# A ring of six gathered rows instead of eight, and its freed weight slot used to keep projection pieces

## The chip, the cores and the metric

The kernel runs on one core of a Trainium2 chip. A core has TensorE (PE, with its weight loads as PEld), VectorE (DVE), ScalarE (ACT), GpSimd (POOL) and SyncE (SP), each with an instruction stream of its own, and 16 DMA engines that all of them share. The metric is the device time of one execution in microseconds.

## What is computed

A first block of two layers and a second block of four, on 256 tokens of 1024 features, all in 32-bit floats. The change lies in the first block, whose layers are an attention, a layer norm, an expert layer and a layer norm. Layer 0 has differential attention with the output projection `w_o_a`, layer 1 stick-breaking attention with `w_o_b`. The expert layer of either one is

```python
def _peer(x, w_pq, sub_keys, u, v):
    q = (xt @ w_pq).reshape(T, PEER_HEADS, 2, PEER_HALF)
    scores = jnp.einsum('thcd,hckd->thck', q, sub_keys)
    ...
    u_sel = jnp.take(u, idb, axis=0)
    h = jax.nn.gelu(jnp.einsum('td,ted->te', xblk, u_sel), approximate=False)
    v_sel = jnp.take(v, idb, axis=0)
    return jnp.einsum('te,ted->td', gb * h, v_sel)
```

So each token takes 128 rows of u and of v, 1024 numbers each, from a table of 16384 experts. The second block (three kinds of attention and a squared-ReLU MLP) follows and is not touched.

## The kernel before, in words

**The expert stage.** The tokens lie in two tiles of 128, and there are two layers, which makes four windows (`WINDOWS`) of 128 picks (`SEL`): 512 picks. For each pick POOL issues one indirect DMA (`gathers`, L2902), which brings for all 128 tokens of the tile the row of u and v of one chosen expert, 128 x 2048 numbers, 1 MB. It goes into the next slot of a ring (`gathered`, `GATHER_SLOTS` = 8). VectorE multiplies the u half by x and sums it (`product`, L2386), ScalarE takes the gelu of two picks at a time (`activate`, L1876), VectorE multiplies it by the gates (L2399), ScalarE writes the two weights as diagonal matrices (`make_diagonal`, L1882), and TensorE adds diagonal times v half to two accumulators (`mix`, L1439), a pair of picks per step. POOL may issue pick n when pick n - 8 is mixed (`value_mixed`), and it issues in order. A window has 64 pairs.

**Work between the pairs.** Every engine runs the same list of pairs, and constants say which other step stands next to which pair. In window 0 that is the attention of layer 0 for the second tile (`second_step`); in windows 1 and 2 the stick-breaking attention of layer 1 for tile 0 and tile 1 (`stick_step`). Windows 0 to 2 also have `late_step`: at pairs 35 to 38 the output projection in four pieces of 256 columns (`s.o`), at 47 to 50 the queries of the next expert layer in four pieces (`s.peer_q`), at 52 its scores. Window 3 has the first input projection of the second block.

**Where weights lie.** `weights` has four slots of 2 MB. The ring of eight takes slots 1 and 2 (two rows each) and four rows in `arena`. Slot 0 is split into two halves for `Piece`, a piece of 1 MB that SP loads shortly before its use and that frees its half when used. Slot 3 holds `KeptPiece`s, first two query pieces of layer 0 (`peer_chunks[1]`), then two output pieces of layer 1 (`kept_o`), loaded once and used for two tiles. `PlacedPiece`s lie in two more places outside of `weights` (`kept_places`): output pieces 2 and 3, of layer 0 and then of layer 1.

**Order of the transfers.** SP issues all weight loads in one fixed order (the function of `@block.sync`), and waits ahead of each for the last user of its place, so one that waits holds up those behind it. `load_stick` loads `Piece`s, `load_kept` the placed ones, `load_chunks` whole chunks. The gathers go out on POOL's queue, at the same 16 DMA engines. `ring_free` says for which projection blocks the first gathers wait, because at the start the ring's places still hold weights of layer 0. At the end of the stage `slot_release` says after which pick each slot takes the first chunks of the second block (the seam); `chunks[1]` (slot 3) is loaded only after the last gather has landed (L1006), and then those of slots 2 and 1 follow (L998).

Of the kernel before, what the change touches and what calls it, by code (L numbers as in the profile page):

```python
# [82 lines left out]


ROW = 2 * D
GATHER_SLOTS = 8
PAIRS = TOPK // 2


# [136 lines left out]
def build(nc, A, out):  # L226
    es = ExitStack()
    with es:
# [24 lines left out]
        arena = sb("arena", [P, 8 * D])  # L253

        in_arena = [arena[:, n * ROW:(n + 1) * ROW] for n in range(4)]
        in_slot = {slot: [weights[:, slot, n * ROW:(n + 1) * ROW] for n in range(2)] for slot in (1, 2)}
        gathered = in_slot[2] + in_arena + in_slot[1]
        assert len(gathered) == GATHER_SLOTS
        o = arena[:, 0:NT * 2 * D].rearrange("p (t d) -> p t d", t=NT)
        bias8 = arena[:, NT * 2 * D:NT * 2 * D + HEADS * T].rearrange("p (h k) -> p h k", h=HEADS)  # L260
# [212 lines left out]
        def in_weights(flat, n, slot, g):  # L473

            slot_uses[slot] += 1
            return halved_chunk(flat, n, weights[:, slot, :], weight_loaded[slot], 16 * slot_uses[slot], (psum_filled[g.bank], g.filled))
# [145 lines left out]
        def column_pieces(flat, first):  # L622

            return [src for src, _, _ in chunks_laid_out(flat, 2 * D, PIECE_COLS)[first:first + 4]]
# [11 lines left out]
        class Second:  # L636
# [3 lines left out]
            def __init__(self):  # L640
                self.t, self.norm, self.keys = 1, (0, 1), 16
                self.block = diff_block(1, 0, 2)
                self.turn = diff_turned(1, (3, 4, 5, 6))
                n = HEADS // 2
                self.probs0, self.done0 = probs_ready.plan(HEADS), unit_done.plan(n)
                self.s, self.turned = [], []
                for j in range(n):
                    self.s.append([group(2 + m) for m in range(2)])
                    self.turned.append(group(4 + j % 2))
                self.values = [group(6 + j % 2, fill=False) for j in range(n // 2)]  # L650
                self.o_turn = maps_turned(1, (4, 5))
                self.out = self.o_turn.done
                half_release[:] = [(psum_filled[self.block[-1].bank], self.block[-1].filled)] * 2
                self.o = [Piece(src, n, 2 + n % 2) for n, src in enumerate(column_pieces(A["w_o_a"][0], 0)[0:2])]
                self.o += [PlacedPiece(n, 1, 2 + n) for n in range(2)]
                self.rows = plan_rows()
                self.peer_turn = Turn(turn_tile(x, xT, 1), (2, 3))
                self.peer_q = [Piece(src, n, 2 + n % 2) for n, src in enumerate(column_pieces(A["peer_w_q"][0], 0)[0:2])]
                self.peer_q += [KeptPiece(peer_chunks[1], n, 2 + n) for n in range(2)]
                self.scores = [group(4 + b) for b in range(4)]  # L660

        class Stick:
# [3 lines left out]
            def __init__(self, t):  # L666
                self.t, self.norm, self.keys, banks = t, (2, t), 32, (2 * t, 2 * t + 1)
                self.n = 4 if t == 0 else 8
                self.log0, self.soft0 = stick_log_ready.plan(self.n), stick_soft_ready.plan(self.n)
                self.e0, self.done0, self.zeroed0 = stick_e_ready.plan(self.n), unit_done.plan(self.n), zeroed.plan(2)  # L670
                self.x_turn = Turn(turn_tile(x, xT, t), banks)
                keys, values = (column_pieces(A["w_kv_b"][0], first) for first in (0, 4))
                queries = column_pieces(A["w_q_b"][0], 0)
                self.k, self.q, self.v, self.pieces = [], [], [], []
                for n in range(4):
                    for kind, src in ((self.k, keys), (self.q, queries), (self.v, values)):
                        kind.append(Piece(src[n], len(self.pieces), banks[0]))
                        self.pieces.append(kind[-1])
                self.s = [group(4 + b % 2) for b in range(self.n)]
                self.later = [group((6, banks[1])[b % 2]) for b in range(self.n)]  # L680
                self.out = [group(7, fill=False) for _ in range(2)]
                first = len(self.pieces)
                self.o = [KeptPiece(kept_o, n, banks[n]) for n in range(2)]
                self.o += [PlacedPiece(n, 2, banks[n]) for n in range(2)]
                self.rows = plan_rows()
                self.peer_turn = Turn(turn_tile(x, xT, t), banks)
                self.peer_q = [Piece(src, first + n, banks[n % 2]) for n, src in enumerate(column_pieces(A["peer_w_q"][1], 0))]
                self.scores = [group(4 + b) for b in range(4)]

            def heads(self, b):  # L690
# [43 lines left out]
        def plan_mixed(w):  # L734

            return [group(2 * (w % NT) + half, fill=False) for half in range(2)]
# [42 lines left out]
        peer_scores += [group(5), group(6)]  # L779


        ring_free = {0: diff_out_blocks[1][-1], 2: later_blocks[4][-1], 4: later_blocks[5][-1], 6: later_blocks[1][-1]}

        ln_root, ln_done = {}, {}
        diff_root = [root_asked.plan()]
# [6 lines left out]
        mixed, ln_in = [plan_mixed(0)], {}  # L792
        second = Second()
        kept_o = in_weights(A["w_o_b"][0], 0, 3, second.peer_q[3].group)
        mixed.append(plan_mixed(1))
        ln_in[EARLY_RUNS[0]] = plan_rows()
        stick = [Stick(0)]
# [6 lines left out]
        for s in late:  # L804
            ln_in[s.norm] = s.rows
        scores_at = [peer_scores] + [s.scores for s in late]
        slot_release[0] = half_release[1 - stick[1].peer_q[0].half]
        kept_until = stick[1].o[1].group
        slot_release[3] = (psum_filled[kept_until.bank], kept_until.filled)
        for slot, buffers in ((1, (6, 7)), (2, (0, 1))):  # L810
            picks = [n for n in range(WINDOWS * SEL) if n % GATHER_SLOTS in buffers]
            slot_release[slot] = (value_mixed.sem, picks[-1] + 1)
        early_normed = y[:, :, 2 * D:3 * D]
        early_in = TileProjection(chunks_laid_out(A["a_w_in"][0], A_IN), (0, 3, 2, 1), (0, 1, 2, 3))
        early_turn = Turn(turn_tile(early_normed, xT, 0), (4, 5))
# [173 lines left out]
        def _(sp):  # L989
# [44 lines left out]
            def load_stick(pieces):  # L1034
                for c in pieces:
                    sp.wait_ge(*c.after)
                    sp.dma_start(c.view, c.src).then_inc(piece_loaded[c.half], 16)
# [34 lines left out]
            load_chunks(peer_chunks)  # L1072
            load_ln_rows()
            sp.wait_ge(x_ready, 1)
            load_kept(0, A["w_o_a"][0], 2)
            queried = peer_q[0]
            sp.wait_ge(psum_filled[queried.bank], queried.filled)
            sp.wait_ge(bias_written, 16)
            load_kept(1, A["w_o_a"][0], 3)
            load_stick(second.o[0:2])  # L1080
            load_stick(second.peer_q[0:2])
            scored = second.scores[3]
            sp.wait_ge(psum_filled[scored.bank], scored.filled)
# [1 line left out]
            for s in stick:  # L1085
                load_stick(s.pieces[0:2])
                if s.t == 0:
                    load_chunks([kept_o])
                    for n in range(2):
                        used = second.o[2 + n].group  # L1090
                        sp.wait_ge(psum_filled[used.bank], used.filled)
                        load_kept(n, A["w_o_b"][0], 2 + n)
                load_stick(s.pieces[2:])
                load_stick(s.peer_q)

            scored = stick[1].scores[3]
            sp.wait_ge(psum_freed[scored.bank], scored.freed)
# [1930 lines left out]
```

## Time and profile before

| | us |
|---|---|
| three runs: median (lowest to highest) | 2735.91 (2732.36 to 2737.7) |
| the profiled execution | 2735.13 |
| its span on the core | 2733.3 |
| TensorE busy in the span | 2513.3 (92%) |
| VectorE busy | 1758.9 (64%) |
| ScalarE busy | 995.4 (36%) |
| GpSimd busy | 651.8 (24%) |
| share of 16 DMA engines taken by POOL's queue | 48.2% |
| share taken by SP's queue | 24.0% |

The span runs from the first to the last instruction of the one execution that was profiled; all durations and instants below are of it. A wait is idle time of an engine, put down to whatever ended it. The landing time of a DMA is counted from the start of its issue to its completion.

### The profile page before, as it was taken

To read this page: it belongs to the slowest core of one execution; us is meant where nothing else is said; L and a number is where in the kernel's file an instruction comes from. 1 tells how busy PE (TensorE), PEld (TensorE's weight loads), DVE (VectorE), ACT (ScalarE), POOL (GpSimd) and SP (SyncE) were. 2 spreads that over 40 slices of the span, in tenths; PEclk is the share of its full clock that TensorE was granted. 3 is DMA by queue.
4 is the path that set the end of the run, shared out by engine and by line. 5 is a ranking of instruction groups with operands and counts; after the bars stand their busy time and mean duration, and the time that the engine had idled before them with its cause. 6 is when DMAs were issued, how large, how long until landed. Compare 5 with 4: busy or idle time off the path is not lost.

```text
span 2733.3 us, 29518 instructions
## 1 busy us (share of the span) xinstructions
PE 2513.3 (92%) x10053; PEld 1581.4 (58%) x10053; DVE 1758.9 (64%) x3966; ACT 995.4 (36%) x2016; POOL 651.8 (24%) x636
## 2 busy tenths in 40 slices
PE   8989897898988899978977899999999999999999
PEld 4544453464553565533422357885688668865787
DVE  2668875756758667678776566554666546647654
ACT  2136332334322354223222144433544444424443
POOL 0134443433434324444444120001000110002000
PEclk9999999999999999999999999999999999999999
DMA  7699999999999999999999734543253405523452
GB/s 296 238 378 415 417 410 402 421 421 421 387 421 421 421 391 406 403 418 421 421 422 421 319 124 154 187 158 147 78 212 140 187 32 204 194 106 124 155 193 98
DMA packets 111344, 791.69 MB, mean 290 GB/s; under 512 B 12979, under 2 KB 15686, under 8 KB 19958
## 3 DMA queue, kind: packets, MB, share of 16 engines
q0 software_dynamic: 74464, 540.07, 48.2%
q1 hardware_dynamic: 36758, 250.10, 24.0%
q8 instruction: 63, 1.03, 0.1%
q14 instruction: 59, 0.48, 0.0%
HBM read 789.05 MB, written 4.22 MB: 290 GB/s over the span
## 4 chain that ended last, share of the span: by engine, by line
PE 65%; DMA 18%; DVE 11%; ACT 3%; issue 2%; POOL 1%; SPq 0%; DVEq 0%; ACTq 0%; POOLq 0%
PE psum L1439 15%; PE psum L1553 13%; PE psum L1160 11%; DMA arena<-in_peer_uv,scratch 10%; PE psum L1510 8%; DMA weights<-in_peer_uv,scratch 7%; PE psum L1512 4%; PE psum L1246 3%; DVE weights L2386 2%; PE psum L1254 2%; DVE arena L2386 2%; PE psum L1232 1%; PE psum L1137 1%; PE psum L1221 1%; PE psum L1208 1%
## 5 line engine op out<-in xcount | busy, mean ns | idle before, releaser
L1439 PE MATMUL psum<-weights,scratch 128*128 128x512 f32 x1024 | 479.4, 615 | 79.0 <-ACT scratch L1882 79.0
L1439 PE MATMUL psum<-arena,scratch 128*128 128x512 f32 x1024 | 476.0, 610 | 74.6 <-ACT scratch L1882 74.4
L2748 DVE TENSOR_TENSOR piece<-weights,piece 128x2048 fp32r<-128x2048 f32 x128 | 292.0, 2292 | 181.1 <-ACT piece L1974 181.1
L2386 DVE SCALAR_TENSOR_TENSOR arena<-arena,x 128x1024 f32<-128x1024 f32 x256 | 309.8, 1223 | 146.5 <-DMA arena<-in_peer_uv,scratch 145.1
L2902 POOL DMA_INDIRECT weights<-in_peer_uv,scratch x256 | 289.0, 1129 | 460.5 <-PE psum L1439 406.0
L2386 DVE SCALAR_TENSOR_TENSOR weights<-weights,x 128x1024 f32<-128x1024 f32 x256 | 309.4, 1225 | 132.4 <-DMA weights<-in_peer_uv,scratch 129.1
L1439 PEld LDWEIGHTS psum<-weights,scratch 128*128 128x128 f32 x1024 | 192.5, 195 | 330.0 <-issue 209.7
L2902 POOL DMA_INDIRECT arena<-in_peer_uv,scratch x256 | 280.3, 1095 | 408.8 <-PE psum L1439 397.3
L1439 PEld LDWEIGHTS psum<-arena,scratch 128*128 128x128 f32 x1024 | 190.9, 193 | 322.5 <-issue 198.8
L1553 PE MATMUL psum<-piece,hidden 128*128 128x512 f32 x1536 | 358.9, 390 | 0.0
L1876 ACT ACTIVATE scratch<-scratch 128x2 f32<-128x2 f32 x255 | 51.9, 203 | 840.2 <-DVE arena L2386 420.4
L1160 PE MATMUL psum<-weights,xT 128*128 128x512 f32 (+2 forms) x792 | 334.4, 576 | 17.7 <-DMA weights<-in_w_qkv_a 8.2
L1553 PEld LDWEIGHTS psum<-piece,hidden 128*128 128x128 f32 x1536 | 284.3, 188 | 59.6
L1510 PE MATMUL psum<-split_x,piece 128*128 128x512 f32 x896 | 318.6, 398 | 0.0
L1974 ACT ACTIVATE piece<-weights 128x2048 fp32r<-128x2048 f32 x128 | 242.7, 1907 | 127.1 <-PE psum L1512 127.1
L1512 PE MATMUL psum<-split_x,piece 128*128 128x256 f32 x896 | 251.5, 281 | 0.0
L1160 PEld LDWEIGHTS psum<-weights,xT 128*128 128x128 f32 x792 | 147.0, 192 | 177.3 <-issue 163.6
L1882 ACT ACTIVATE scratch<-const,scratch 128x128 f32<-128x128 f32 x512 | 178.0, 394 | 63.8 <-DVE scratch L2399 57.0
L1510 PEld LDWEIGHTS psum<-split_x,piece 128*128 128x128 f32 x896 | 168.4, 188 | 41.1
L1512 PEld LDWEIGHTS psum<-split_x,piece 128*128 128x128 f32 x896 | 169.2, 189 | 2.0
L1993 ACT ACTIVATE hidden<-scratch 128x512 fp32r<-128x512 f32 x64 | 40.5, 632 | 218.3 <-DVE scratch L2769 198.8
L1246 PEld LDWEIGHTS psum<-xT,weights 128*128 128x128 f32 x896 | 105.7, 194 | 17.0 <-issue 16.3
(273 smaller groups left out, 2686.8 us busy)
## 6 DMA issues: line engine op xcount, KB each, us to landing
weights<-in_w_up SPq DMA_DIRECT2D x64, 1024.0 KB, 4.8
weights<-in_w_down SPq DMA_DIRECT2D x64, 1024.0 KB, 4.8
weights<-in_w_kv_b SPq DMA_DIRECT2D x16, 1024.0 KB, 9.4
weights<-in_peer_w_q SPq DMA_DIRECT2D x10, 1024.0 KB, 9.2
weights<-in_a_w_in SPq DMA_DIRECT2D x5, 2048.0 KB, 11.5
weights<-in_w_q_b SPq DMA_DIRECT2D x8, 1024.0 KB, 9.2
weights<-in_a_w_out SPq DMA_DIRECT2D x4, 2048.0 KB, 8.6
weights<-in_w_qkv_a SPq DMA_DIRECT2D x3, 2048.0 KB, 16.9
```

The source lines that it names most:

```text
L1160: mm = pe.matmul(psum[g.bank][:, 0:w], source[:, block0 + k, t * P:(t + 1) * P], c.columns(k, c0, w), start=(k == 0), stop=(k == c.rows - 1))
L1246: mm = pe.matmul(to[:, j * P:(j + 1) * P], c.columns(k, j * P, P), xT[:, k, t * P:(t + 1) * P], start=(k == 0), stop=(k == KB - 1))
L1254: mm = pe.matmul(to[:, 0:PIECE_COLS], xT[:, k, t * P:(t + 1) * P], c.columns(k), start=(k == 0), stop=(k == KB - 1))
L1439: mm = pe.matmul(psum[g.bank][:, :], diagonal[:, n % DIAGONALS, :], row[:, D + half * BANK:D + (half + 1) * BANK], start=(k == 0), stop=(k ...
L1510: pe.matmul(psum[g.bank][:, 0:2 * T], w[0][:, k, b * P:(b + 1) * P], split_x_pair[:, k, :, :], start=(k == 0), stop=False)
L1512: mm = pe.matmul(psum[g.bank][:, 0:T], w[1][:, k, b * P:(b + 1) * P], split_x[0][:, k, :], start=False, stop=(k == KB - 1))
L1553: mm = pe.matmul(psum[g.bank][:, :], h[a][:, k, t * P:(t + 1) * P], w[c][:, k, half * BANK:(half + 1) * BANK], start=(first and k == 0 and ...
L1882: act.activation(diagonal[:, n % DIAGONALS, :], identity, ACT.Copy, scale=weight[:, k:k + 1])\
L1974: act.activation(split_piece[n][0][:, :], raw_piece[n], ACT.Copy).then_inc(high_ready.sem, 1)
L2386: dve.scalar_tensor_tensor(u, u, 1.0, x[:, n // SEL % NT, :], ALU.mult, ALU.mult, accum_out=dots[:, n % SEL:n % SEL + 1]).then_inc(dotted. ...
L2748: dve.tensor_tensor(split_piece[n][1][:, :], raw_piece[n], split_piece[n][0][:, :], ALU.subtract)\
L2902: pool.indirect_dma_start(gathered[n % GATHER_SLOTS], None, rows, bass.IndirectOffsetOnAxis(ap=expert[:, w % NT, k:k + 1], axis=0), elemen ...
```

## The change

The ring has six rows: four in `arena` and two in slot 1. Slot 2 is no longer part of it and holds two pieces, each used more than once. At first it keeps output columns 512 to 1023 of layer 0 (`diff_out_chunks[1]`, which was loaded there for tile 0 anyway) for the second tile as well; the two places outside take output pieces 0 and 1 instead of 2 and 3, and the two `Piece` loads of pieces 0 and 1 go. After the last of them is used, SP loads query pieces 0 and 1 of the second expert layer into slot 2 (`kept_q`, one transfer of 2 MB, ahead of `kept_o`); both stick tiles use them, and only query pieces 2 and 3 are still loaded per tile. Before, each tile loaded all four. POOL waits for pick n - 6 instead of n - 8. The first gathers wait for `later_blocks[4]`, `[5]` and `[1]`. At the end slot 2 is free when the second tile's query piece 1 is used, and slot 1 at the last pick of ring places 4 and 5, pick 509, for which it waits until 510 picks are mixed; before, these were 512 mixed for slot 1 and a late pick for slot 2.

```diff
-GATHER_SLOTS = 8
+GATHER_SLOTS = 6
...
-        in_slot = {slot: [weights[:, slot, n * ROW:(n + 1) * ROW] for n in range(2)] for slot in (1, 2)}
-        gathered = in_slot[2] + in_arena + in_slot[1]
+        in_slot = [weights[:, 1, n * ROW:(n + 1) * ROW] for n in range(2)]
+        gathered = in_arena + in_slot
...
-                self.o = [Piece(src, n, 2 + n % 2) for n, src in enumerate(column_pieces(A["w_o_a"][0], 0)[0:2])]
-                self.o += [PlacedPiece(n, 1, 2 + n) for n in range(2)]
+                self.o = [PlacedPiece(n, 1, 2 + n) for n in range(2)]
+                self.o += [KeptPiece(diff_out_chunks[1], n, 2 + n) for n in range(2)]
...
-                self.peer_q = [Piece(src, first + n, banks[n % 2]) for n, src in enumerate(column_pieces(A["peer_w_q"][1], 0))]
+                self.peer_q = [KeptPiece(kept_q, n, banks[n]) for n in range(2)]
+                self.peer_q += [Piece(src, first + n, banks[n]) for n, src in enumerate(column_pieces(A["peer_w_q"][1], 0)[2:4])]
...
-        ring_free = {0: diff_out_blocks[1][-1], 2: later_blocks[4][-1], 4: later_blocks[5][-1], 6: later_blocks[1][-1]}
+        ring_free = {0: later_blocks[4][-1], 2: later_blocks[5][-1], 4: later_blocks[1][-1]}
...
+        kept_q = in_weights(A["peer_w_q"][1], 0, 2, second.o[3].group)
...
-        slot_release[0] = half_release[1 - stick[1].peer_q[0].half]
+        slot_release[0] = half_release[stick[1].peer_q[3].half]
...
-        for slot, buffers in ((1, (6, 7)), (2, (0, 1))):
-            picks = [n for n in range(WINDOWS * SEL) if n % GATHER_SLOTS in buffers]
-            slot_release[slot] = (value_mixed.sem, picks[-1] + 1)
+        queried_until = stick[1].peer_q[1].group
+        slot_release[2] = (psum_filled[queried_until.bank], queried_until.filled)
+        in_slot_1 = [n for n in range(WINDOWS * SEL) if n % GATHER_SLOTS in (4, 5)]
+        slot_release[1] = (value_mixed.sem, in_slot_1[-1] + 1)
...
-            load_kept(0, A["w_o_a"][0], 2)
+            load_kept(0, A["w_o_a"][0], 0)
...
-            load_kept(1, A["w_o_a"][0], 3)
-            load_stick(second.o[0:2])
+            load_kept(1, A["w_o_a"][0], 1)
...
-                    load_chunks([kept_o])
+                    load_chunks([kept_q, kept_o])
                     for n in range(2):
-                        used = second.o[2 + n].group
+                        used = second.o[n].group
...
-                load_stick(s.peer_q)
+                load_stick(s.peer_q[2:])
```

## Rows read from the trace of the kernel before

**Rows 1.** The page: its head, and GB/s in 40 equal slices of the span

```profile
span 2733.3 us, 29518 instructions
...
GB/s 296 238 378 415 417 410 402 421 421 421 387 421 421 421 391 406 403 418 421 421 422 421 319 124 154 187 158 147 78 212 140 187 32 204 194 106 124 155 193 98
```

**Rows 2.** Windows: busy us of each engine, granted clock, DMA share, GB/s; 150:1530

```profile
150.00:1530.00 1380.00, 1210.59 (x3997) 633.45 (x3996) 987.25 (x2522) 463.68 (x1105) 563.92 (x507) 0.98 1.01 413
```

**Rows 3.** Waits, 123:1545: engine and line, releaser, us in total, times, longest

```profile
DVE arena L2386 <- DMA arena<-in_peer_uv,scratch: 145.1, 123, 3.4
...
DVE weights L2386 <- DMA weights<-in_peer_uv,scratch: 129.1, 107, 3.7
...
PE psum L1439 <- ACT scratch L1882: 153.4, 110, 6.2
```

**Rows 4.** Timeline, 1521:1544: start us, us, engine, line, op, out<-in

```profile
1523.66 0.94 POOL L2902 DMA_INDIRECT arena<-in_peer_uv,scratch  x1 [0.78 <-PE psum L1439]
...
1524.64 3.70 PE L1439 MATMUL psum<-weights,scratch 128*128 128x512 f32 x8 [1.25 <-ACT scratch L1882]
...
1528.61 0.94 POOL L2902 DMA_INDIRECT weights<-in_peer_uv,scratch  x1 [0.78 <-PE psum L1439]
...
1537.40 1.23 DVE L2386 SCALAR_TENSOR_TENSOR arena<-arena,x 128x1024 f32<-128x1024 f32 x1 [1.25 <-DMA arena<-in_peer_uv,scratch]
...
1539.56 3.70 PE L1439 MATMUL psum<-arena,scratch 128*128 128x512 f32 x8 [1.28 <-ACT scratch L1882]
```

**Rows 5.** Source L2902, seven windows starting at 122, 180, 340, 400, 700, 960, 1080

```profile
DMA to landing us min/median/max: 5.5/11.6/16.9
DMA to landing us min/median/max: 6.6/10.2/13.9
DMA to landing us min/median/max: 6.7/8.7/11.3
DMA to landing us min/median/max: 5.6/9.5/13.4
DMA to landing us min/median/max: 5.5/8.6/12.6
DMA to landing us min/median/max: 7.3/9.5/13.6
DMA to landing us min/median/max: 5.7/8.4/10.7
```

**Rows 6.** Timeline, POOL, 735:748; landings of the gathers issued at 727.6, 737.3, 743.2

```profile
737.32 1.05 POOL L2902 DMA_INDIRECT weights<-in_peer_uv,scratch  x1 [0.30 <-issue]
...
743.18 0.93 POOL L2902 DMA_INDIRECT arena<-in_peer_uv,scratch  x1 [2.26 <-issue]
...
DMA to landing us min/median/max: 7.4/7.4/7.4
DMA to landing us min/median/max: 9.2/9.2/9.2
DMA to landing us min/median/max: 8.3/8.3/8.3
```

**Rows 7.** Source L2902, three windows: 1120:1190, 1200:1290, 750:900

```profile
DMA to landing us min/median/max: 9.7/14.3/18.6
DMA to landing us min/median/max: 9.6/12.6/13.7
DMA to landing us min/median/max: 11.1/13.5/19.4
```

**Rows 8.** Timeline, SP (its DMA issues), 100:1560

```profile
162.00 1.02 SPq L1037 DMA_DIRECT2D weights<-in_w_o_a  x2
...
424.43 0.44 SPq L998 DMA_DIRECT2D weights<-in_w_o_b  x1
...
646.05 127.95 SPq L1037 DMA_DIRECT2D weights<-in_peer_w_q  x4
```

**Rows 9.** Windows, columns as in rows 2; 765:790

```profile
765.00:790.00 25.00, 25.00 (x141) 17.90 (x140) 9.68 (x18) 3.49 (x12) 7.63 (x7) 1.00 1.01 420
```

## The prediction

> **What bounds the kernel now.** I read the page's head and its line of GB/s first. The span is 2733.3 us, and from the third to the twenty-second of the forty slices the DMA engines move 378 to 422 GB/s, mostly 421; before and after they move far less [rows 1]. That plateau is the expert stage, in which 512 gathers of 1 MB each (a row of u and v per token) pass through the ring. Over its inner 1380 us the engines are busy for 1.01 of the time, at 413 GB/s, while TensorE is busy 1210.59 us [rows 2]. So 421 GB/s is the ceiling here, one gather (1.05 MB) costs 2.49 us of it, a pair 4.98 us, and the stage is 8/421, or 1.9%, from the ceiling. The list of waits agrees: VectorE stands 145.1 + 129.1 us for gathers that have not landed, TensorE 153.4 us for the diagonals that follow from them [rows 3]. TensorE is a close second, so there are places where it leads and the DMA follows; the change has to be read there.
>
> **The loop through the ring.** The timeline of the quiet end of the stage shows one turn. A gather is issued at 1523.66; its product starts at 1537.40, as soon as it has landed, 13.74 us after the issue; its pair is mixed from 1539.56 for 3.70 us, to 1543.26, which is 5.86 us after the landing. An earlier pair's mix ends at 1528.34 (1524.64 + 3.70), and the next issue into the slot that it freed is at 1528.61, 0.27 us later [rows 4]. The turn is 13.74 + 5.86 + 0.27 = 19.87 us, four pairs of 4.97 us. Of the 13.74 us most is waiting behind other gathers: a gather into an empty queue lands in 5.5 us (the first line of [rows 5]), its pair's second, issued just behind it, in 7.4 [rows 6]. That surplus is what eight slots buy.
>
> **Six slots in the steady part.** The turn becomes three pairs, 14.91 us, and leaves 14.91 - 5.86 - 0.27 = 8.8 us for the landing of a pair's second gather. Enough? The nearest rows are a place where the queue had just run low: seconds issued at 737.32 and 743.18 land after 9.2 and 8.3 us, at 746.5 and 751.5, 5.0 us apart [rows 6], which is the full rate. So 8.8 us keeps the pace, and I charge the steady part 0. Lower bound 0 (the ceiling is not lifted); upper bound, if 9.2 were needed instead of 8.8, 0.4 us for each 14.9 us over some 700 us of steady stretches: 19 us.
>
> **Six slots where the queue runs low.** When TensorE or VectorE leads for a while, gathers land sooner and sooner after their issue, since slots come back late. The lowest landing time of a stretch less the 5.5 us of an empty queue is its spare; two slots fewer take one pair, 4.98 us, from it, and what is missing is time in which the DMA engines stand still. After each such stretch the DMA leads again, so it is not won back. The stretches from 122, 180, 340, 400, 700, 960 and 1080 us have minima, in that order, of 5.5, 6.6, 6.7, 5.6, 5.5, 7.3 and 5.7 [rows 5]. Without the first, the losses are 3.9 + 3.8 + 4.9 + 5.0 + 3.2 + 4.8 = 25.6 us. Two milder ones, from 1120 and 1200, have 9.7 and 9.6 (the first two lines of [rows 7]): 0.8 + 0.9 = 1.7. Together 27.3 us. Each term lies between 0 (the dip was TensorE's to lose) and 4.98.
>
> The stretch from 180 to 300 deserves more. Its median landing is 10.2 us (second line of [rows 5]), not 13.7: the second tile's attention holds the rows some 3.5 us longer in every turn. A turn of 14.9 us less that longer hold (19.9 - 10.2 = 9.7) leaves 5.2, under both 5.5 and 7.4. At 1.3 us missing (to 6.5, the middle of those two) in eight turns of 14.9 us it would lose 10 us, against 3.9 charged; VectorE's own work hides part of it. I take 8, that is 4 more; bounds 0 and 6 more.
>
> **Loads taken away and moved.** All pass through the same engines, 2.49 us per MB. (a) The two output pieces loaded at 162.00 [rows 8] are no longer needed: 5.0 us less. They follow the first dip (5.5 us at the start of the stage, where two rows fewer are fetched ahead, a loss of 5.0), and the next dip comes from 180 on. The gain and the first dip's loss cancel: 0. The first gather also starts later, after the block for which the third used to wait, which no row prices; the same head start of the DMA covers it, or it falls in that term. (b) SP now issues kept_q (2 MB) next to kept_o in the burst that begins around 424.43 [rows 8]. It is waited for by its queries only some 300 us on, but it goes through full engines just when that burst already holds the gathers back, and SP has nothing else queued behind it but the rest of the burst: +5.0 us, bounds 0 and 5.0. (c) Of each of the two sets of four query pieces of the second expert layer (the third line of [rows 8] is the first set, 646.05 to 774) two go, 5.0 us of engine time each. The last two of the set stood in the query steps around 766, where TensorE is busy 25.00 of 25.00 us with the DMA still at 420 GB/s [rows 9]. There the ring is full, and what the loads leave free the gathers can't use beyond the spare. The minimum from 750 to 900 is 11.1 (third line of [rows 7]), a spare of 5.6: 4.98 of the ring and 4.98 saved leave 4.4 idle, a net gain of 0.6. In the second set (stretch from 1120, spare 4.2) saving 5.0 makes 5.0 more idle: 0. So 4 MB fewer buy 0.6 us there; bounds 0 and 10.
>
> **Edits at nothing.** The output pieces in the kept places and in slot 2 have landed long before use (the former second set did the same); TensorE's waits for them are on semaphores already reached. If that cover failed, it would stand one landing of a loaded queue, 9 to 14 us, once. The instructions on all engines and their order stay. At the seam the last weight chunk is freed by pick 510 instead of 512; SP issues it at most one mix, 3.70 us [rows 4], earlier, but behind two chunks on the same engines: 0, bounds -2 and 0.
>
> **The sum.** 27.3 + 4.0 + 0 + 5.0 - 0.6 + 0 = 35.7 us. The profiled execution took 2735.13 us (span 2733.3 and 1.8 around it), 0.8 below the median of the runs shown, 2735.91: 2735.1 + 35.7 = 2770.8, rounded to 2771 us.
>
> **A rule against this.** The rows put an unloaded gather at 5.5 us. The Trainium skill, "DMA: Bandwidth & Descriptors", section "Anatomy of one DMA — SWDGE (gpsimd) path", gives about 2.0 us plus the bytes at 436 GB/s, 4.4 us for 1 MB. By that rule a pair in flight would hide the fixed part and six slots would be ample; every dip would have 1.1 us more to spare, which lowers the sum by some 8 us. The rows, 5.5 and 7.4, are of this access and decide. The rule's own outcome is rival 1.
>
> **Rivals.** (1) The queue never really empties: six slots cover the landing everywhere, the dips belong to TensorE and not to the DMA, and the stage simply moves 4 MB less: 4 x 2.49 = 10 us, 2725 us. It decides if the GB/s in the dips stay as they are. For it: the engines' share stays near 1.00 even in most dips. Against it: landing times of 5.5, 5.6 and 5.7 us are those of an empty queue, and the GB/s fell to 387 and 391 in such slices [rows 1]. Chance 0.07. (2) About half of the dips are given back, since TensorE leads on both sides of them, and kept_q hides: 27.3/2 + 4 - 3 (part of the saved loads) = about 15 us, 2750 us. For it: the dips of 340 and 400 lie close together, as do those of 960 and 1080. Chance 0.17. (3) The steady part starves too, since a turn has no room for VectorE's routing steps: the 19 us bound above on top of the sum, 2790 us. For it: the margin is 8.8 against 8.3 to 9.2. Against it: the steady row of seconds at 8.3 keeps the pace. Chance 0.16. (4) Gains and losses cancel: loads save 10, dips cost 10, 2735 us. Chance 0.04. The forecast keeps 0.56.
>
> **How the numbers follow.** A measurement of this kernel can't tell less than about 0.2% (5.5 us) from no change. Faster 0.07 is rival 1, same 0.04 rival 4, slower 0.89 the rest. The range: from 2747 (rival 2 less 3 us) to 2800 (rival 3 with the upper bound of the attention stretch and some of the dips at 4.98); rivals 1 and 4 and the tail above 2800 are left out, under 2 in 10.
>
> **What would show it.** The profile after should have the same instructions and busy times, a stage longer by 30 to 40 us with about 4 MB less, so GB/s near 400 instead of 413; landing times with minima of 5.5 in all of the dips and steady ones of 8 to 9 instead of 13 us; steady pairs still 4.97 us apart. Behind the seam nothing changes. Landing minima well above 5.5 in the dips would prove rival 1 or 2; steady pairs of 5.1 us or more rival 3. The forecast is wrong if the stage's length moves by under 10 us although the landing times fall to 5.5, or if kept_q's burst stretches nothing.

## The result, and the profile after

The changed kernel takes 2831.92 us, the median of four runs (2826.11 to 2838.07), beside 2735.81 us for the kernel before (2732.36 to 2737.7): a ratio of 1.0356, interval 1.0337 to 1.0374. The change makes the kernel 96 us slower; forecast were 36 us slower, and the time lies 32 us above the range. The execution that was profiled took 2838.07 us, with a span of 2836.2 us, 102.9 more than before [rows 1].

The page of the changed kernel: its head, the granted TensorE clock and the GB/s in 40 slices, and the two groups of the mixing matmuls.

```profile
span 2836.2 us, 29513 instructions
...
PEclk9988899899999999999999999999999999999999
...
GB/s 286 246 317 336 354 343 373 404 407 417 377 367 398 385 395 390 353 370 400 385 399 415 414 202 119 208 177 141 84 191 192 105 90 192 180 143 119 134 192 104
...
L1441 PE MATMUL psum<-arena,scratch 128*128 128x512 f32 x1368 | 665.5, 633 | 139.0 <-ACT scratch L1884 137.6
...
L1441 PE MATMUL psum<-weights,scratch 128*128 128x512 f32 x680 | 324.6, 622 | 64.8 <-ACT scratch L1884 64.6
```

The plateau of 421 GB/s of [rows 1] is gone: slices 3 to 7 are at 317 to 373. The work is the same: 2048 matmul records of the mix before and after. But they are busy 665.5 + 324.6 = 990.1 us, where the page of the kernel before has 479.4 + 476.0 = 955.4, and the clock digit falls to 8 in four of the first eight slices.

Windows over the whole expert stage, first the changed kernel, then the one before (columns as in [rows 2]):

```profile
123.00:1648.00 1525.00, 1285.70 (x4145) 664.41 (x4144) 1017.11 (x2591) 471.81 (x1130) 591.52 (x516) 0.96 0.96 379
```

```profile
123.00:1547.00 1424.00, 1250.05 (x4146) 654.78 (x4144) 1010.76 (x2589) 474.29 (x1130) 572.89 (x516) 0.98 1.00 410
```

The DMA engines move 379 instead of 410 GB/s, over 1525 instead of 1424 us. The list of waits for the stage, changed kernel, answers [rows 3]:

```profile
DVE arena L2388 <- DMA arena<-in_peer_uv,scratch: 266.8, 211, 4.4
...
PE psum L1441 <- ACT scratch L1884: 202.1, 120, 5.2
...
DVE weights L2388 <- DMA weights<-in_peer_uv,scratch: 126.9, 98, 3.7
```

VectorE waits 266.8 + 126.9 = 393.7 us for rows, 119.5 more than before; TensorE waits 202.1 us for diagonals, 48.7 more. The chain at the seam (the hand-over from the last gathers to the first weights of the second block) shows that the difference ends there; first after, then before:

```profile
1645.96 11.58 DMA weights<-in_a_w_in
...
1657.59 2.84 PE psum L1162 x6
```

```profile
1543.16 11.49 DMA weights<-in_a_w_in
...
1554.69 7.13 PE psum L1160 x16
```

The first projection behind the gathers starts at 1657.59 and at 1554.69, 102.9 us apart, which is the whole difference of the spans. So the question is one of the stage alone.

**The quiet end.** The timeline of the changed kernel answers [rows 4]:

```profile
1572.00 3.70 PE L1441 MATMUL psum<-arena,scratch 128*128 128x512 f32 x8 [1.62 <-ACT scratch L1884]
...
1575.97 0.94 POOL L2904 DMA_INDIRECT arena<-in_peer_uv,scratch  x1 [0.78 <-PE psum L1441]
...
1584.76 1.22 DVE L2388 SCALAR_TENSOR_TENSOR arena<-arena,x 128x1024 f32<-128x1024 f32 x1 [1.25 <-DMA arena<-in_peer_uv,scratch]
...
1586.91 3.70 PE L1441 MATMUL psum<-arena,scratch 128*128 128x512 f32 x8 [1.27 <-ACT scratch L1884]
...
1590.89 0.94 POOL L2904 DMA_INDIRECT arena<-in_peer_uv,scratch  x1 [0.78 <-PE psum L1441]
```

A mix ends at 1575.70, its slot is issued into at 1575.97, the product of that row starts at 1584.76, its pair is mixed to 1590.61, and at 1590.89 the slot is issued into again. The turn is 14.92 us, three pairs of 4.97; from issue to product it is 8.79 us where it was 13.74. This is the forecast's steady turn to the tenth of a us. Most of the loss lies elsewhere.

**Where it lies.** The table takes the ends of the mixes from both traces and divides by pairs (a window is 64 pairs); the next columns are means over the second gathers of the pairs, from the start of the issue to the start of the product, and from there to the end of the mix.

| pairs | us a pair, before | after | issue to product, before | after | product to mixed, before | after |
|---|---|---|---|---|---|---|
| 8 to 32 | 5.17 | 6.05 | 11.7 | 9.2 | 8.4 | 8.8 |
| 32 to 56 | 5.23 | 6.15 | 11.5 | 8.9 | 10.1 | 9.2 |
| 64 to 104 | 5.97 | 6.12 | 15.1 | 10.1 | 8.3 | 8.0 |
| 104 to 128 | 5.27 | 5.62 | 13.4 | 9.4 | 7.4 | 6.9 |
| 128 to 168 | 6.07 | 6.35 | 13.8 | 9.9 | 10.0 | 8.8 |
| 168 to 192 | 5.30 | 5.76 | 13.6 | 9.8 | 7.5 | 6.9 |
| 192 to 224 | 4.98 | 5.26 | 13.2 | 9.3 | 6.3 | 6.1 |
| 224 to 250 | 5.02 | 5.08 | 13.8 | 9.0 | 5.9 | 5.9 |

The rows of the table follow one identity: issue to product, plus product to mixed, plus about 0.4 us to the next issue, is 4 pairs before and 3 pairs after. For pairs 8 to 32 after that is 9.2 + 8.8 + 0.4 = 18.4, beside 3 x 6.05 = 18.2. The rows agree to some 0.3 us, but for pairs 32 to 56 before, 1 us off, since their turns end in the slower pairs behind. The identity holds whatever sets the pace, because POOL issues as soon as a slot is free. So it says how the parts of a turn add up and not which of them is the cause; that is what the experiments are for.

Pairs 56 to 64, beside SP's burst of loads, take 6.90 us before and 7.10 after. By window the loss is 55.4, 14.1, 21.9 and 11.4 us; the forecast had 21.6, 4.4, 8.8 and 0.9.

A piece of the attention stretch in the changed kernel, timeline from 231 to 266:

```profile
237.18 1.72 POOL L2904 DMA_INDIRECT weights<-in_peer_uv,scratch  x1 [0.78 <-PE psum L1441]
...
243.90 8.90 PE L1441 MATMUL psum<-arena,scratch 128*128 128x512 f32 x16
...
247.59 1.22 DVE L2388 SCALAR_TENSOR_TENSOR weights<-weights,x 128x1024 f32<-128x1024 f32 x1 [1.20 <-DMA weights<-in_peer_uv,scratch]
...
247.93 1.70 POOL L2904 DMA_INDIRECT arena<-in_peer_uv,scratch  x1 [9.04 <-PE psum L1441]
...
254.69 3.70 PE L1441 MATMUL psum<-weights,scratch 128*128 128x512 f32 x8
...
258.67 1.57 POOL L2904 DMA_INDIRECT weights<-in_peer_uv,scratch  x1 [0.78 <-PE psum L1441]
...
260.36 5.40 PE L1441 MATMUL psum<-arena,scratch 128*128 128x512 f32 x8 [1.97 <-ACT scratch L1884]
```

The gather issued at 237.18 is multiplied 10.4 us later, at 247.59, and mixed from 254.69 to 258.39, 10.8 us after that: TensorE mixes two pairs in one go (243.90, 8.90 us), then has attention steps, then mixes again. So slots come back in bunches: after 9.04 us in which POOL had none, it issues at 247.93. At 258.67 the slot of the gather of 237.18 is issued into again, a turn of 21.5 us. And the mix at 260.36, before which TensorE stood idle for 1.97 us, takes 5.40 us instead of 3.70: the granted clock over these 5.40 us is 0.68 of full speed, part of them at the lower level.

### The profile page after: what moved, and what is told of

Read it like the earlier page. It is cut to its first block, busy times and chain, and to the rows that moved or that the text cites. A ratio compares the mean times of both kernels' runs of the same rounds, so it can differ in the third digit from the quotient of the medians.

```text
span 2836.2 us, 29513 instructions
## 1 busy us (share of the span) xinstructions
PE 2549.8 (90%) x10053; PEld 1591.1 (56%) x10053; DVE 1764.7 (62%) x3966; ACT 993.4 (35%) x2016; POOL 670.4 (24%) x636
## 4 chain that ended last, share of the span: by engine, by line
PE 64%; DMA 19%; DVE 10%; ACT 4%; issue 2%; POOL 1%; SPq 0%; DVEq 0%; ACTq 0%; POOLq 0%
PE psum L1441 15%; DMA arena<-in_peer_uv,scratch 13%; PE psum L1555 12%; PE psum L1162 11%; PE psum L1512 7%; DMA weights<-in_peer_uv,scratch 5%; PE psum L1514 4%; PE psum L1248 3%; DVE arena L2388 3%; PE psum L1256 2%; PE psum L1139 1%; DVE weights L2388 1%; PE psum L1234 1%; ACT scratch L1884 1%; PE psum L1223 1%
## 5 line engine op out<-in xcount | busy, mean ns | idle before, releaser
L1441 PE MATMUL psum<-arena,scratch 128*128 128x512 f32 x1368 | 665.5, 633 | 139.0 <-ACT scratch L1884 137.6
L2388 DVE SCALAR_TENSOR_TENSOR arena<-arena,x 128x1024 f32<-128x1024 f32 x342 | 416.1, 1224 | 269.5 <-DMA arena<-in_peer_uv,scratch 266.8
L2904 POOL DMA_INDIRECT arena<-in_peer_uv,scratch x342 | 394.3, 1153 | 671.4 <-PE psum L1441 621.5
L1441 PEld LDWEIGHTS psum<-arena,scratch 128*128 128x128 f32 x1368 | 264.5, 201 | 490.2 <-issue 285.3
L1441 PE MATMUL psum<-weights,scratch 128*128 128x512 f32 x680 | 324.6, 622 | 64.8 <-ACT scratch L1884 64.6
L2388 DVE SCALAR_TENSOR_TENSOR weights<-weights,x 128x1024 f32<-128x1024 f32 x170 | 206.6, 1224 | 128.5 <-DMA weights<-in_peer_uv,scratch 126.9
L1441 PEld LDWEIGHTS psum<-weights,scratch 128*128 128x128 f32 x680 | 128.8, 197 | 237.8 <-issue 136.2
L2904 POOL DMA_INDIRECT weights<-in_peer_uv,scratch x170 | 193.5, 1138 | 287.2 <-PE psum L1441 267.8
```

The source lines that it names most:

```text
L1441: mm = pe.matmul(psum[g.bank][:, :], diagonal[:, n % DIAGONALS, :], row[:, D + half * BANK:D + (half + 1) * BANK], start=(k == 0), stop=(k ...
L2388: dve.scalar_tensor_tensor(u, u, 1.0, x[:, n // SEL % NT, :], ALU.mult, ALU.mult, accum_out=dots[:, n % SEL:n % SEL + 1]).then_inc(dotted. ...
L2904: pool.indirect_dma_start(gathered[n % GATHER_SLOTS], None, rows, bass.IndirectOffsetOnAxis(ap=expert[:, w % NT, k:k + 1], axis=0), elemen ...
```

## Experiments

All kernels differ from the one before or from the changed one by what their diff shows; where the depth of the ring changes, the lines that fit `ring_free` and `slot_release` to it are left out in part. Theory A, the turn: the time of a pair is the larger of the DMA ceiling and the turn of a slot divided by the pairs in the ring, where the turn has a landing part that can't shrink at will.

### The ring alone, and the loads alone

Six rows with the old loads, slot 2 idle:

```diff
-GATHER_SLOTS = 8
+GATHER_SLOTS = 6
...
-        gathered = in_slot[2] + in_arena + in_slot[1]
+        gathered = in_arena + in_slot
...
+        slot_release[2] = (psum_filled[diff_out_blocks[1][-1].bank], diff_out_blocks[1][-1].filled)
```

> The ring alone: six rows, and every weight load of the kernel before, in its old order and place; slot 2 stays idle in the stage. Theory A (turn): each slot now goes once through issue, landing, product, mixing in a turn that two fewer slots can no longer hide, and the time is the ring's alone: 2827 to 2837 us, with window 0 at 6.0 to 6.2 us a pair as in the changed kernel. Theory B (loads): kept_q's 2 MB in the burst near 424 us and the new places of the pieces cost what the forecast had not counted, so the ring alone is near the forecast: 2760 to 2780 us.

Measured 2835.18 us (2834.3 to 2836.07), ratio 1.0368 (1.0348 to 1.0389): the loss of the changed kernel, whole. In windows, 190 to 480 us, of before, the changed kernel and this one:

```profile
190.00:480.00 290.00, 252.37 (x822) 130.14 (x821) 217.80 (x576) 106.00 (x250) 119.77 (x106) 0.95 1.01 412
```

```profile
190.00:480.00 290.00, 250.24 (x797) 130.88 (x798) 193.82 (x499) 98.55 (x231) 110.85 (x94) 0.91 0.89 343
```

```profile
190.00:480.00 290.00, 247.12 (x798) 129.86 (x797) 192.99 (x495) 98.46 (x231) 107.99 (x95) 0.92 0.90 349
```

412 GB/s fall to 343 and 349, with about as many matmuls (822, 797 and 798 records). Two rows fewer are enough for the loss; the loads that were moved and saved are not needed for it.

The other half, eight rows and 6 MB fewer loads:

```diff
-                self.o = [Piece(src, n, 2 + n % 2) for n, src in enumerate(column_pieces(A["w_o_a"][0], 0)[0:2])]
+                self.o = [PlacedPiece(n, 1, 2 + n) for n in range(2)]
...
-                self.peer_q = [Piece(src, first + n, banks[n % 2]) for n, src in enumerate(column_pieces(A["peer_w_q"][1], 0))]
+                self.peer_q = [KeptPiece(kept_o, n, banks[n]) for n in range(2)]
+                self.peer_q += [Piece(src, first + n, banks[n]) for n, src in enumerate(column_pieces(A["peer_w_q"][1], 0)[2:4])]
...
-            load_stick(second.o[0:2])
...
-                load_stick(s.peer_q)
+                load_stick(s.peer_q[2:])
```

> The ring of eight with 6 MB of weight loads left out: the two output pieces of the diff layer and query pieces 0 and 1 of both stick tiles are not loaded, and the pieces already kept in their places are multiplied instead, so these columns of the output are computed from other weights. Theory A: such loads go where the ring is full or are absorbed by the next dip, 2725 to 2736 us. Rival: every MB is worth its 2.49 us in a stage that is bound by the DMA engines, 6 x 2.49 = 15 us, 2721 us or less.

Measured 2729.17 us (2725.72 to 2734.06), ratio 0.9982 (0.9972 to 0.9992): 5 us won (2.2 to 7.7) of the 15 that 6 MB take on the engines. The rival is out: loads that go out while the ring is full or ahead of a dip are worth about a third of their engine time together (a seventh to a half by the interval). What each of them is worth was not measured.

### Are the eight places or the waits of the ring what counts?

```diff
-                    if n >= GATHER_SLOTS:
-                        pool.wait_ge(value_mixed.sem, n - GATHER_SLOTS + 1)
-                    elif n in ring_free:
+                    if n >= GATHER_SLOTS - 2:
+                        pool.wait_ge(value_mixed.sem, n - (GATHER_SLOTS - 2) + 1)
+                    if n < GATHER_SLOTS and n in ring_free:
```

> The kernel before with its eight places, each gather still going where it went, but POOL waits until pick n - 6 is mixed instead of n - 8; all loads as before. Theory A (turn): the depth is what is waited for, so 2825 to 2840 us. Rival (fewer places in weights and more traffic in arena, or the later first gathers, cost part of it): clearly under 2820 us.

Measured 2831.45 us (2828.25 to 2834.64), ratio 1.035 (1.0329 to 1.0371). With every row in the place it had before and two gathers fewer on their way, the loss is all there. Neither the places nor the later start of the first gathers is needed for it, to within the some 5 us of the interval: over 190 to 480 us this kernel too moves 351 GB/s, with the engines busy 0.90 of the time.

### Seven rows and four

```diff
-GATHER_SLOTS = 8
+GATHER_SLOTS = 7
...
-        gathered = in_slot[2] + in_arena + in_slot[1]
+        gathered = in_slot[2][0:1] + in_arena + in_slot[1]
```

> The ring alone with seven rows, loads as before. Theory A (turn): a pair costs the larger of what it costs with eight rows and the turn divided by 3.5; the turn of the attention stretch is about 18.3 us in the changed kernel, 5.23 us a pair against 5.2 with eight rows, so seven rows lose little: 2740 to 2765 us. Rival (each dip loses what a row is worth, in proportion): half of what six rows lose, about 2784 us.

Measured 2761.8 us (2759.51 to 2764.1), ratio 1.01 (1.008 to 1.012): the seventh row is worth 73 us of the 100, the eighth 27. The loss is not in proportion.

```diff
-GATHER_SLOTS = 8
+GATHER_SLOTS = 4
...
-        gathered = in_slot[2] + in_arena + in_slot[1]
+        gathered = in_arena
```

> The ring alone with four rows. Theory A (turn): a pair costs half a turn. The part of the turn behind the start of the product and the issue was 9.1 to 9.5 us in the attention stretch, 8.4 and 9.2 in windows 1 and 2 and 6.5 in the quiet end with six rows; with a landing of 7.4 us for a pair in an empty queue that is 8.3, 7.9 to 8.3 and 7.0 us a pair, 465 us more than the changed kernel in the sum: 3250 to 3350 us. The forecast's own rule (each dip costs at most one more pair of rows, 4.98 us, and the steady part nothing down to an empty queue's landing) would give some 2890 us.

Measured 3317.94 us in one run. The turn gave 3250 to 3350, the forecast's own rule 2890. The single stretches scatter more than the sum: pairs 8 to 32 take 9.02 us and pairs 32 to 56 7.80, where 8.3 were expected for both. The same window (190 to 480) for seven and for four rows:

```profile
190.00:480.00 290.00, 244.43 (x808) 126.29 (x807) 207.20 (x544) 105.02 (x246) 116.75 (x102) 0.97 0.98 392
```

```profile
190.00:480.00 290.00, 192.86 (x488) 98.12 (x488) 145.68 (x381) 78.71 (x175) 64.88 (x66) 0.80 0.66 246
```

392 GB/s with seven, 246 with four, where the DMA engines work 0.66 of the time and the granted clock is 0.80. In the quiet end (pairs 224 to 250) the trace has 7.06 us a pair: 6.9 from issue to product, 6.9 on to the mixed pair and 0.4, half of a turn of some 14.1. From issue to product is now near the 7.4 us of [rows 6], and 7.0 to 8.2 in the stretches before; with six rows its mean never came under 8.9 in any row of the table. That is the number that the forecast had wrong.

### A delay that takes no DMA time

```diff
+                if n >= (WINDOWS - 1) * SEL and n % 2 == 0:
+                    for _ in range(4):
+                        act.wait_ge(act_step, then(act.activation(diagonal[:, n % DIAGONALS, :], identity, ACT.Copy,
+                                                                  scale=weight[:, k:k + 1])))
```

It stands in `make_diagonal` ahead of the real one; the result is the same. In the trace it is 1.70 us a pair (timeline of the ring of eight: the added writes, then the mix behind them):

```profile
1495.38 1.70 ACT L1884 ACTIVATE scratch<-const,scratch 128x128 f32<-128x128 f32 x4 [0.23 <-DVE scratch L2403]
...
1497.57 3.70 PE L1439 MATMUL psum<-weights,scratch 128*128 128x512 f32 x8 [1.27 <-ACT scratch L1886]
```

With eight rows:

> The kernel before, with a delay on ScalarE ahead of the first diagonal of each pair in window 3: the same diagonal is written four times more, each waited for, some 2 us a pair in all. It lengthens the way of every row from its landing to its mixing, and takes no DMA time and no time of TensorE. Theory A (turn): with eight rows the turn of the quiet end (19.9 us) holds a landing time of 13.7 us, of which an empty queue needs 7.4, so 2 us are hidden: 2733 to 2741 us. Rival (a delay on the way to the mix costs its length, or a fixed part of it, whatever the ring): 64 x 2 = 128 us or a large part of it, in both rings alike.

Measured 2734.52 us (2732.41 to 2743.14), ratio 0.9995 (0.9985 to 1.0005): nothing, for 64 x 1.7 = 109 us of added delay. With six rows:

> The changed kernel with the same delay in window 3. Theory A (turn): with six rows the turn is 14.9 us and its landing part 9.0, near its floor, so of each 2 us at least 0.4 and at most 2 come through, a third of them on every pair: 8 to 43 us more than the changed kernel, 2840 to 2875 us, while the same delay costs the ring of eight nothing. Rival (the steady part is bound by the DMA engines at either depth, as the forecast had it, and has room for 2 us): 2828 to 2836 us.

Measured 2863.37 us (2862.76 to 2874.91), ratio 1.048 (1.0454 to 1.0505): 31 us more than the changed kernel, 0.49 us for each of 64 pairs, a little under a third of 1.7 (0.57). Windows in the quiet end, eight rows (1420 to 1520) and six (1560 to 1640):

```profile
1420.00:1520.00 100.00, 75.06 (x160) 29.23 (x159) 63.54 (x145) 55.81 (x149) 48.47 (x41) 0.98 1.01 421
```

```profile
1560.00:1640.00 80.00, 59.42 (x114) 23.41 (x112) 44.41 (x99) 39.16 (x106) 32.12 (x29) 0.89 0.92 361
```

421 GB/s stand against 361. Without the delay the changed kernel has, at 1520 to 1600:

```profile
1520.00:1600.00 80.00, 58.52 (x128) 22.86 (x128) 51.73 (x120) 19.29 (x54) 34.65 (x32) 1.00 1.01 410
```

This is the cleanest test: the same 1.7 us is free in one ring and costs nearly its third in the other, so the steady part had almost no room left at six rows, though it ran near the full pace without the delay. Over window 3 of the traces, product to mixed grew from 6.0 to 8.0 us and issue to product shrank from 9.2 to 8.7: 0.5 us of room, and no more. Some 0.2 us of the growth are the mixes, 4.01 instead of 3.77 us at a granted clock of 0.89 instead of 1.00 in the two windows above. By the same third up to 0.1 of the 0.49 us a pair may be the clock and not the delay.

### Mixing first

TensorE mixes a pair before the step beside it and not after it (the same edit in both rings):

```diff
                     for pair in range(PAIRS_IN_TILE):
+                        mix(w, pair)
                         if w == 0:
                             second_step(second, pair)
...
-                        mix(w, pair)
```

> The changed kernel, but TensorE mixes a pair before the other step that stands next to it and not after it; the same instructions otherwise. Theory A: the time from product to mixing (8 to 10 us in windows 0 to 2) falls toward the 5.9 us of the quiet end, the turn shortens by 1 to 3 us in windows 0 to 2 and a third of that is won for each of their 192 pairs: 2740 to 2800 us. Rival (the dips are TensorE's own work, whose amount is unchanged): 2825 us or more, since the order of TensorE's work doesn't change its sum.

Measured 2819.82 us (2814.48 to 2825.17), ratio 1.0312 (1.0284 to 1.034): 12 us better than the changed kernel (the two intervals just overlap) and 15 better than the ring alone, which ran beside it, and between the two expectations. In window 0 the theory holds: product to mixed falls from 8.8 to 6.1 us for pairs 8 to 32, the pair from 6.05 to 5.39, and 26 us are won by pair 64. In the window of 190 to 480 us:

```profile
190.00:480.00 290.00, 245.12 (x819) 127.29 (x820) 206.96 (x539) 104.36 (x246) 115.25 (x101) 0.96 0.96 383
```

383 GB/s instead of 343. But pairs 64 to 104 then take 6.30 instead of 6.12, and 14 of the 26 us are gone at the end of the stage. In pairs 64 to 104 and 128 to 168 product to mixed falls little (7.6 instead of 8.0, 7.8 instead of 8.8), and issue to product grows by 0.8 us in both.

With eight rows, in all windows and then in window 0 alone (`if w == 0` before the new line, `if w > 0` before the old one):

> The kernel before (eight rows), TensorE mixing a pair before the step that stands next to it, in all windows. Theory A (turn): with eight rows the DMA ceiling of 4.98 us a pair is met nearly everywhere, so of the shorter turn only what window 0 stands above the ceiling can come back, 0.2 us in each of 48 pairs, and windows 1 and 2 may lose a little as they did with six rows: 2722 to 2738 us. Rival (the earlier release of the slots is worth the same with eight rows as with six, 12 us or more): 2722 us or less.

Measured 2751.71 us (2749.99 to 2755.78), ratio 1.0065 (1.0044 to 1.0086): slower, and a miss for both expectations. The sum of the turn doesn't change (20.65 us for pairs 8 to 32, 20.48 before): what is cut from product to mixed comes back from issue to product, as it must where the turn doesn't set the pace. That it loses 17 us is not explained by the turn: pairs 128 to 168 take 6.20 instead of 6.07, and pairs 168 to 192 5.48 instead of 5.30, 9 of the 15 us by which the stage ends later in the trace. Presumably the steps put back keep VectorE or ScalarE waiting; that was not tried.

> The same with the mix first in window 0 alone, where it gained 25 us with six rows, and the old order in windows 1 to 3. Theory A (turn and ceiling): 2722 to 2732 us, up to 12 us won in window 0 and no loss behind it. Rival (the gain of window 0 is given back behind it, since SP's burst of loads near 430 us then meets a stage that is further along): 2733 to 2738 us.

Measured 2739.3 us (2734.71 to 2741.96), ratio 1.0009 (0.9989 to 1.0029): no difference, and just above both expectations. The up to 12 us of window 0 don't show: by pair 64 the trace is 4 us behind the kernel before, with 6.3 us instead of 8.4 from product to mixed and 14.0 instead of 11.7 from issue to product in pairs 8 to 32. No version here that computes the same result beats the kernel before.

### The load moved out of the burst

```diff
-                    load_chunks([kept_q, kept_o])
+                    load_chunks([kept_o])
...
                 load_stick(s.pieces[2:])
+                if s.t == 0:
+                    load_chunks([kept_q])
```

> The changed kernel with kept_q (2 MB) loaded behind the stick pieces of tile 0 and not in the burst near 430 us. If the burst is what the load costs (pairs 56 to 64 took 7.10 us each in the changed kernel and 6.06 in the ring of six with the old loads, 8 us in all), this gives 2822 to 2828 us. If the engines' time is the same wherever it is taken, 2829 to 2835 us.

Measured 2838.56 us (2831.72 to 2843.71), ratio 1.0387 (1.0361 to 1.0412), which overlaps the changed kernel's 1.0337 to 1.0374 and is not faster. Pairs 56 to 64 do fall from 7.10 to 6.07 us, 8 us in all, but the 192 pairs behind take 1109 us instead of 1101 in the traces (pairs 168 to 192 take 5.87 instead of 5.76, pairs 224 to 250 5.26 instead of 5.08). The profiled execution here, 2831.72 us, is the fastest of its four and that of the changed kernel, 2838.07, the slowest of its four, so the traces differ by 6 us before the burst as well, where the edit can't act. So the burst's cost is seen where it stands and, by the medians, not in the total; with executions some 12 us apart, what gives it back was not settled.

## Why the prediction was wrong

The direction was right and the steady turn too; the size was not. The forecast charged each dip once, with at most 4.98 us, and it charged a turn as a whole only in one stretch, with a landing of 6.5 us. The runs showed a charge on every pair of the stretches with a long hold (the way from landing to mixed), with some 9 us from issue to product.

- **The bound, and the steady turn**: right. 14.92 us and 4.97 us a pair at the quiet end, as computed; 0 charged, and pairs 224 to 250 lost 1.6 us in all. But "enough" was only just enough: the delay of 1.7 us shows that almost nothing is left (31 us against 0). Pairs 192 to 224 lost 9 us, where 0.9 were charged.
- **The loss in a dip, at most 4.98 us for each**: the step that failed first. A dip was taken as one emptying of a store, after which the DMA is behind by two rows and no more. But the turn binds on every pair, as long as it is longer than three times the pace. The loss grows with the length of a stretch: 0.88 us for each of 24 pairs, 0.92 for the next 24, 43 us in all, where the dips from 180, 340 and 400 and the extra for attention were charged 16.6. Four rows make it plain: 3318 us, where the rule gives 2890.
- **The attention stretch**: the mechanism was written down (a turn too long by the hold), and two terms of its sum were mis-sized; the landing is the one that matters most. The landing was taken as 6.5 us, the middle of 5.5 and 7.4 in an empty queue; the trace has 9 us from issue to product with six rows, even at 343 GB/s. The timeline from 237 suggests why (argued, no run isolates it): slots come back in bunches, and the last of a bunch waits behind the others while the engines later stand idle. And eight turns were counted, for 180 to 300 us, where pairs 8 to 56 are sixteen. The turn grows past three pairs at the old pace (15.6 us) by 2.7 us, times 16 turns 43 us. How much hangs on the landing can be worked out from the table's columns of before: four times the pace, less issue to product, plus the landing, divided by three. With 7.4 us this gives 5.5 and 5.6 us for the two attention rows, 16 us lost there and nothing in any other row. With 9 us it gives 6.0 and 6.1, and 81 us over all rows of the table, which lost 90.
- **The start**: charged 0, measured 10.6 us by pair 8. The forecast had let 5.0 us lost and 5.0 us saved cancel. The ring alone, with all loads, lost 9.2 us by pair 8 and is within 2 us of the changed kernel by pair 32, so the two saved output pieces bought next to nothing there; the eight places with the wait for n - 6, whose first six gathers wait as before, lost 8.0.
- **Loads**: 5 us for 6 MB with eight rows. The forecast's own terms for the same 6 MB, with six rows, are 5.6 (5.0 for the output pieces, 0.6 for the query pieces), which fits as a sum and was not tested in its parts; the full engine time, the 4 x 2.49 = 10 us of rival 1, is ruled out. With six rows the changed kernel and the ring alone are 3 us apart, inside their intervals. The 5.0 us for kept_q, also their upper bound, were too small in their place (8 us in pairs 56 to 64) and don't show in the sum: with the load elsewhere the time is the same.
- **The seam**: right, 0.
- **The rivals**: rival 3 was the nearest, a turn without room, but it was put in the steady part and priced at 19 us. Its place was wherever TensorE or VectorE holds a row longer than 6 us. What would have shown the place in advance is the turn of each stretch, read from its own rows, as worked out above. The 9 us that it needs are a reading of the changed kernel; the rows of before had 8.3 and 9.2 us for seconds at the full rate [rows 6], and the forecast used these for the steady part alone. They are no fixed floor either: 8.7 with the delay, 6.9 to 8.2 with four rows.
- **The rule of the Trainium skill** in "DMA: Bandwidth & Descriptors", "Anatomy of one DMA — SWDGE (gpsimd) path", 4.4 us for a transfer of this size, was rightly set aside: the trace has 5.5 us for a gather into an empty queue [rows 5], and the shortest mean from issue to product in any stretch here is 6.9 us, with four rows.
- **What the forecast lacked altogether** is the clock. TensorE's granted clock over 190 to 480 us was 0.95 with eight rows, 0.91 with six and 0.80 with four; the records show stretches at half speed (1.2 of 2.4 GHz) after it stood idle, and a mix there takes 5.40 us and not 3.70. The 34.7 us by which the mixes grew are part of the turn; a third of them, 12 us, may be in the loss. That is argued from the rows; no run separates it. With seven rows the clock was 0.97, no lower than with eight, and 27 us were lost all the same: the clock is not what makes a shallower ring slow, though it may add to it.

## What to carry to other kernels

A ring of buffers has a turn: issue to landing, landing to use, use to the next issue. Divide it by the depth for every stretch of the kernel, with that stretch's own hold and with the landing time that a shallow ring really shows (with six rows here 9 us, not the 5.5 to 7.4 of an empty queue), and compare it with the pace of the bound; where it is longer, every item pays. Eight rows looked generous at the quiet end, where even 1.7 us of delay per pair is free; it is the stretches with a long hold that use them, and the bytes saved elsewhere were worth about a third of their time in this stage.

## What was not expected of the hardware

How far the DMA engines are from 421 GB/s over the same 290 us (190 to 480) depends on the depth: 412 GB/s with eight rows, 392 with seven, 343 with six, 246 with four. What was not expected is that the way from issue to product hardly shortens when the engines have time to spare: with six rows, busy 0.89 of the time, it is still 9 us, and with four rows, busy 0.66, it is 8.2. And TensorE, which waits more for rows, is granted less clock: 0.80 of full speed over these 290 us with four rows, and in its whole stage 37 of the 256 pairs are mixed in 5.4 us and not in 3.7. That the slower mixes lengthen the turn in their turn follows from the identity; how much of the loss it makes was not measured.
